# Weighting gathered experts in four 64x64 quarters of the TensorE array

## What is computed

```
s1, s2 = q[:, :, 0] . sub_keys[:, 0], q[:, :, 1] . sub_keys[:, 1]
t1, i1 = top_k(s1, 16); t2, i2 = top_k(s2, 16)
top, pos = top_k(t1 + t2, 16)          # 16 experts of each of 8 heads
g = softmax(top)
act = gelu(einsum('td,tkd->tk', u, up[eidx]))
y = einsum('tk,tkd->td', g * act, down[eidx])
```

## Time and profile before

| | before |
|---|---|
| median of 3 runs | 4607.52 us (4603.65 to 4612.15) |
| profiled execution | 4609.56 us |
| its span | 4607.8 us |
| PE busy | 3903.4 us, 85% |
| DVE busy | 3237.5 us, 70% |
| POOL busy | 1524.9 us, 33% |
| ACT busy | 796.7 us, 17% |
| HBM read | 1477.87 MB, 321 GB/s over the span |

### The profile page before, as it was taken

One profiled execution on the slowest core, in us unless ns is written; L12 is line 12 of the kernel. 1 busy time (PEld: TensorE's weight loads), 2 busy tenths in 40 slices (PEclk: granted clock), 3 DMA queues, 4 the chain that ended last, 5 costly groups with the idle time before them and its releaser, 6 DMA issues.

```text
span 4607.8 us, 46202 instructions
## 1 busy us (share of the span) xinstructions
PE 3903.4 (85%) x11216; PEld 1862.7 (40%) x11216; DVE 3237.5 (70%) x8467; ACT 796.7 (17%) x2152; POOL 1524.9 (33%) x1425
## 2 busy tenths in 40 slices
PE   8998897888888888888888879989788888888887
PEld 3435754333333333333333334466433333333332
DVE  3106746888888888888888743075688888888885
ACT  1002321111111111111111111133111111111111
POOL 1100102444444444444444410000244444444442
PEclk9998899999999999999999999979999999999999
DMA  7632125999999999999999951122599999999998
GB/s 270 215 112 62 65 96 223 427 421 413 414 422 402 424 427 398 423 419 385 427 408 408 427 211 55 53 74 101 213 421 427 405 416 427 390 421 427 402 427 343
DMA packets 243743, 1486.01 MB, mean 323 GB/s; under 512 B 25120, under 2 KB 49952, under 8 KB 72848
## 3 DMA queue, kind: packets, MB, share of 16 engines
q0 software_dynamic: 191232, 1385.58, 72.7%
q1 hardware_dynamic: 52368, 98.79, 6.5%
HBM read 1477.87 MB, written 2.21 MB: 321 GB/s over the span
## 4 chain that ended last, share of the span: by engine, by line
PE 38%; DMA 29%; DVE 15%; issue 13%; POOL 2%; ACT 1%; DVEq 1%; POOLq 0%; SPq 0%; ACTq 0%; PEldq 0%
DMA arena<-in_updown,arena 28%; PE ps L786 12%; PE ps L778 5%; PE ps L623 4%; PE ps L638 3%; PE ps L747 3%; POOL arena L1084 2%; DVE arena L1441 2%; DVE arena L1450 2%; PE ps L643 2%; PE ps L716 2%; PE ps L672 1%; PE ps L618 1%; PE ps L705 1%; PE ps L574 1%
## 5 line engine op out<-in xcount | busy, mean ns | idle before, releaser
L786 PE MATMUL ps<-arena 128*128 128x512 f32 x5120 | 2419.6, 611 | 534.2 <-DVE arena L1441 529.1
L1084 POOL DMA_INDIRECT arena<-in_updown,arena x1280 | 1444.5, 1128 | 2099.3 <-PE ps L786 1610.6
L1450 DVE CUSTOM_DVE_ANT_0 arena<-arena 128x1024 bf16<-128x1024 f32 x1280 | 1566.4, 1224 | 289.5 <-DMA arena<-in_updown,arena 247.3
L786 PEld LDWEIGHTS ps<-arena 128*128 128x128 f32 x5120 | 919.7, 191 | 1982.8 <-DVE arena L1441 1138.3
L999 ACT ACTIVATE arena<-arena 128x1 f32<-128x1 f32 x1280 | 259.2, 203 | 2669.7 <-DVE arena L1450 2649.2
L1441 DVE TENSOR_SCALAR arena<-CN,arena 128x128 f32<-128x128 f32 x1280 | 444.0, 347 | 224.2 <-PE ps L786 196.8
L778 PE MATMUL ps<-arena 128*128 (+1 forms) x1280 | 297.8, 387 | 18.5 <-DVE arena L1382 16.1
L778 PEld LDWEIGHTS ps<-arena 128*128 128x128 f32 x1280 | 249.2, 195 | 87.7 <-issue 36.2
L1071 POOL TENSOR_TENSOR arena<-arena 128x256 f32<-128x256 f32 x64 | 40.4, 663 | 662.3 <-DMA arena<-in_bias 662.3
L623 PE MATMUL ps<-arena 128*128 128x512 f32 (+1 forms) x672 | 236.7, 509 | 0.0
L623 PEld LDWEIGHTS ps<-arena 128*128 128x128 f32 x672 | 126.8, 192 | 114.0 <-issue 103.1
(11 more groups left out here) (195 smaller groups left out, 2777.5 us busy)
## 6 DMA issues: line engine op xcount, KB each, us to landing
arena<-in_ada_w POOLq DMA_DIRECT2D x40, 1024.0 KB, 5.3
arena<-in_updown,arena POOLq DMA_INDIRECT x1280
arena<-in_wq SPq DMA_DIRECT2D x32, 512.0 KB, 4.2
arena<-in_w_in SPq DMA_DIRECT2D x6, 2048.0 KB, 10.4
arena<-in_w_in SPq DMA_DIRECT2D x24, 512.0 KB, 3.9
arena<-in_ada_w SPq DMA_DIRECT2D x4, 2048.0 KB, 14.3
arena<-in_bias SPq DMA_DIRECT2D x16, 512.0 KB, 4.0
arena<-in_w_out SPq DMA_DIRECT2D x2, 4096.0 KB, 12.9
```

Of the source, the lines that this page charges most:

```text
L786: mm = e.matmul(ps[hf][:], diag[:, k % 2, :], ring[:, k % RING, D + hf * 512:D + (hf + 1) * 512], start=False, stop=False, skip_group_chec ...
L1084: e.indirect_dma_start(ring[:, k % RING, :], None, updown, bass.IndirectOffsetOnAxis(ap=idx16[:, k:k + 1], axis=0)).then_inc(sem(f"rows{k ...
L1450: e.tensor_tensor_reduce(prod[:, k % 2, :], ring[:, k % RING, 0:D], u, 1.0, 0.0, ALU.mult, ALU.add, dots[:, k:k + 1]).then_inc(sem("L.dot_ ...
```

## The change

`weigh` splits each slot into four matmuls of 64x64 by 512 columns: token half `g` by column half `hf`. The operand `diag` is now 128x64: since the identity has nothing off its diagonal, the two 64x64 blocks on it are enough, one per token half, each on its own 64 partitions. Quarter (g, hf) reads the partitions of token half g and writes the partitions of column half hf in bank g. So the sums lie otherwise in PSUM: `ps[g]` holds token half g, its lower 64 partitions columns 0 to 511 and its upper 64 columns 512 to 1023. The copy to `ysb` undoes this in four activations of 64x512. `id64` is two 64x64 identities above each other, built once in each layer. `weigh` also raises a semaphore (`pe_token`) between its wait and its matmuls. The last of the four matmuls still raises `L.slot_done` for each slot.

```diff
-        diag = r(2, P)
+        diag = r(2, HALF)
+        id64 = r(HALF)
...
                     e.wait_ge(sem("L.diag_ready"), n + (k + 1))
-                    for hf in range(2):
-                        mm = e.matmul(ps[hf][:], diag[:, k % 2, :], ring[:, k % RING, D + hf * 512:D + (hf + 1) * 512],
-                                      start=False, stop=False, skip_group_check=True)
+                    e.sem_inc(sem("pe_token"), 1)
+                    for g in range(2):
+                        rows = slice(g * HALF, (g + 1) * HALF)
+                        for hf in range(2):
+                            mm = e.matmul(ps[g][hf * HALF:(hf + 1) * HALF, :], diag[rows, k % 2, :],
+                                          ring[rows, k % RING, D + hf * 512:D + (hf + 1) * 512],
+                                          start=False, stop=False, skip_group_check=True)
...
-                    for hf in range(2):
-                        ins = e.activation(ysb[:, hf * 512:(hf + 1) * 512], ps[hf][:], ACT.Copy)
+                    for g in range(2):
+                        for hf in range(2):
+                            ins = e.activation(ysb[g * HALF:(g + 1) * HALF, hf * 512:(hf + 1) * 512], ps[g][hf * HALF:(hf + 1) * HALF, :], ACT.Copy)
...
-                        e.tensor_scalar(diag[:, k % 2, :], ident, acts[:, k:k + 1], gate_all[:, bass.ds(slot * UN + k, 1)], ALU.mult, ALU.mult).then_inc(sem("L.diag_ready"), 1)
+                        e.tensor_scalar(diag[:, k % 2, :], id64, acts[:, k:k + 1], gate_all[:, bass.ds(slot * UN + k, 1)], ALU.mult, ALU.mult).then_inc(sem("L.diag_ready"), 1)
...
+                    lc.link(e.tensor_tensor(id64, ident[:, 0:HALF], ident[:, HALF:P], ALU.add))
```

More of the change, by code:

```diff
@@ L45 @@
 RING = 8
+HALF = P // 2
 EXP_AT, NORM_AT = 11, 14
```

## The result

| | before | after |
|---|---|---|
| median of 14 runs each | 4607.6 us (4601.2 to 4613.7) | 4616.8 us (4609.5 to 4622.5) |
| ratio | | 1.0021, 95% interval 1.0013 to 1.0030 |
| profiled execution, span | 4607.8 us | 4612.9 us |
| PE busy | 3903.4 us | 3478.1 us |

What follows compares the result with a forecast made beforehand. DMA bounds the two expert stages, with 95 us of shortfall against 427 GB/s. Boundaries -12, loop boundaries -3, first tiles -2, layer ends +4 sum to -13 us: 4595 us from 4607.5, range to hold 8 in 10 4550 to 4618.

Steps and rivals of the forecast that it cites:

- The quarters run side by side: Weighting on PE: all four quarters run at once, 1.07 us per slot for 1.98, some 1.9 at half clock.
- The clock falls: Expert stages: PE would work 44%, so the first half of each unit runs at 1.2 GHz; key scores some 5 us.
- The diagonal: DVE's tensor_scalar on half the columns: some 280 ns for 347, 0.07 us less per slot, 0.5 us earlier at step 8.
- The copies: ACT's copy out at each tile end: four activations at 0.5 us each instead of two, +1.0 us.
- the sum: Forecast case, chance 0.62: effects at tile boundaries at the low clock plus first tiles and layer ends, -13 us in all.
- The knot's first half: Tile boundary: closing and opening matmuls at half clock, 1.88 to 3.6 and 1.98 to 3.6 us, delaying the next tile's releases.
- the second rival: The knot at the tile boundary tightens: first releases 4.4 us later instead of 1.1, 20 us slower, 4628 us; chance 0.18.
- The step that failed: Behind the key scores DVE stops waiting for PE, is caught up by the second unit: -1.4 and -0.7 us at later holes.
- the 8 starts behind a boundary: Tile starts following another tile: -1.5 us each, together -12 us, and perhaps 3 more at two behind loops over tiles.
- The first rival: Expert stages: the clock stays up with the quarters, the late gather comes some 3 us earlier, 55 us gained, 4552 us; chance 0.16.
- The signs named in the forecast: If right: weighting 1.1 and 1.9 us, clock 0.55 to 0.75, copies 2.1 us, DMA 415 to 417 GB/s, POOL waiting for PE.
- The sign for the whole being wrong: Over the kernel: the time moves while the DMA windows don't; no size given.

Runs made afterwards that it cites:

- e3: Kernel before with its copy of the sums cut into four activations of 64x512, nothing else: 4616.6 us, ratio 1.0022.
- e1: Changed kernel plus matmuls of zeros behind most slots and the closing matmuls, to keep PE busy and the clock up: 4596.8 us, ratio 0.9976.
- e8: Changed kernel with the zeros of e1 and two copies of 128x512 for four of 64x512, output in wrong places: 4584.7 us, ratio 0.9955.
- e13: Changed kernel with the key scores between steps 11 and 12 instead of 7 and 8, nothing else: 4572.7 us, ratio 0.9930.
- e4_before_token: Kernel before with only the semaphore step put between PE's wait and the weighting's matmuls: 4606.1 us, ratio 0.9998.
- e12: e13 with the gelus of the next tile's first two slots ahead of the copy on ACT: 4580.5 us, ratio 0.9947.

## Why the prediction was wrong

- *The quarters run side by side: right.* A slot takes 1.09 us at full clock and 1.98 to 1.99 at half, forecast 1.07 and 1.9.
- *The clock falls: right.* 0.72 over both stages, forecast 0.55 to 0.75. The key scores take 5.06 us in the boundary shown, forecast some 5.
- *The diagonal: small miss.* 317 ns for 280 forecast, from 347. The forecast drew its line through the 210 ns of the earlier trace rows, a single record; the 80 records of that line have a median of 329 ns. What the 37 ns are worth in time no run shows.
- *The copies: their length right, their price too low.* Four take 2.40 us for 1.09, +1.3 where +1.0 was forecast. Counted at 8 us for the boundaries in the sum, they cost 10 and 12 us at the high clock (e3; e1 less e8) and 5 at the low one.
- *The knot's first half happened.* The opening matmuls took 3.42 us and not 1.98; the sum had them unchanged and left that to the second rival. The closing ones took 1.98 us, where the sum had 1.3 us more for them. From the start of the closing matmuls DVE's restart comes 1.6 us later and the first gather 2.2 us later than before, between the 1.1 of the sum and the 4.4 of the rival. DVE's wait behind the copy, 1.96 us, did not pass the 3 us that the rival named as its sign.
- **The step that failed** is the sentence "Behind the key scores DVE no longer waits 2.15 us and its small sequels for PE, so it is caught up when the second unit begins: about -1.4 us at the second hole and -0.7 at the third". The sum took the key scores' extra length as +1.3 us for one slot of one unit per tile and let the faster draining pay it back. In the trace DVE waited 3.18 us there, and so in every unit of the tile, 2.9 us on average for 2.0 before: the slow key scores return in every unit, and the sum had a price for one. It also contradicts itself: it has the slot of step 8 done 0.5 us later behind the key scores, and it is for this slot that DVE waits. The start of the tile made the forecast kind of gain, 0.7 us of the 1.5; the rest of the tile lost 1.5. e13 shows the step from the other side: with the key scores moved to where DVE is not dense and the clock is mostly up, DVE's wait goes to 21.8 us and the gain comes, 33 us against before.
- *The sum, term by term.* By the start times of the gathers in the two traces, the 8 starts behind a boundary gained 7.5 us where 15 were forecast (12, and 3 behind the loops), the rest of these tiles lost some 6 where nothing was forecast, the first tiles of the two layers lost 3.9 where 2 were to be gained, and the ends of the layers lost 4.2 us, forecast 4. These are single executions; e4_before_token, which takes the same time as before, has 5 us less in the same 8 starts, so the gain there may be smaller still.
- *The first rival was mis-sized.* Its mechanism is real (e1 and e8 are faster than before), but its price of 55 us was 10 in e1, 22 with two copies. It took nearly the whole shortfall of 95 us against 427 GB/s for late gathers. The best kernel, e13, with almost no wait of DVE for PE, moves 420 GB/s over the stage and not 427. So 1917 x (1 - 420/427) = 31 us of the first stage's 59 stay where DVE hardly waits for PE any more. The DMA share there is 1.01, so most of this is a full queue that moves a little less, and the forecast had 30 us for such stretches and the filling in both stages together.
- *The signs named in the forecast.* The weighting, the clock and POOL's wait came out as named for the forecast being right, the copies at 2.40 us for 2.1, and the DMA at 414 and 416 GB/s for 415 to 417. That last sign couldn't decide: one GB/s over both stages is 7.8 us, nearly the whole difference. The sign for the whole being wrong, a time that moves while the DMA windows don't, came out within this rounding.

The Trainium skill (TensorE: Matmul & The Clock Gate, Part 1) says that activity releases the clock. The runs here agree: the same quarters had a mean clock of 0.78 without and 0.97 with matmuls of zeros beside them.

## What to carry to other kernels

Making one user of TensorE cheaper can lower its clock and so lengthen its other users: ask of each of those whether somebody dense waits behind it, in every repetition and not only at the worst place. Before giving up such a change, move the slowed work to a stretch where its waiters have slack, or where the engine has just been busy and the clock is up again; here both held at once, and a change that cost 9 us came to gain 21 by that alone. A head start for one engine is worth nothing where the next engine of the chain becomes late by it.

## What the hardware showed

- Four float32 quarters of 64x64 by 512 columns overlap at both clock levels: 8 records in 1.09 us at the upper one, as 8 records of column groups in 1.07 us, and in 1.98 us at the lower. A full 128x512 pair takes 1.98 us at the upper and up to 3.78 us where the clock is down (the opening matmuls of e12).
- The quarters lowered the granted clock: 0.72 over the stages for 0.99 before.
- ScalarE's copy from PSUM takes the same for 64 partitions as for 128, 592 and 594 ns for 512 columns.
- A `tensor_scalar` on VectorE with half the columns (64 for 128) takes 317 ns for 347.
- Keeping the clock up by matmuls of zeros was worth 20 us at one placement of the key scores and cost 11 at another, where 16 key score matmuls took 3.72 us without them.
